# The dense residual moved from the end of the second expert pass to its start, and new places in the order of the delta-rule stage

## The chip, the cores and the metric

The kernel runs on one core of one Trainium2 chip. The metric is the time of one execution on the device, in microseconds (us). A trace of one profiled execution gives every instruction with its start, its length and what its engine waited for.

## The reference

One step of a decoder trunk for 528 prompt tokens (16 of them learned meta tokens) and 8 sequences of 4 new tokens, 560 token columns in all, width 1024, all in fp32:

```
h = h + W_out(concat[GDN(xn), Conformer(xn)])        xn = RMSNorm(h)
h = h + PEER(RMSNorm(h))                             16384 single-neuron experts
y = RMSNorm(h, final_norm_w)                         meta tokens dropped
PEER:  act = gelu(x . u[e]);  y = sum over heads, top 16:  gate * act * v[e]
```

GDN is a gated delta rule with 4 heads of 128, done in chunks: in each a unit triangular system of 128 x 128 is solved per head, with a state matrix handed from chunk to chunk. Conformer is a gated depthwise convolution of 31 taps with a layer norm. PEER scores 128 x 128 product keys in 8 heads and takes the best 16 of each.

## The kernel before, in words

Engines: TensorE (PE) multiplies, VectorE (DVE) and ScalarE (ACT) read its results from PSUM (8 banks), GpSimd (POOL) helps and issues gathers, SyncE (SP) issues all other DMAs in program order.

**Projections and delta stage (to about 457 us).** Weights come in blocks; each is split into a high and a low fp32r part and multiplied in three products. From the ninth block on, the projections share the engines with the delta stage: five chunks (chunk 0 of 48 rows, chunks 1 to 4 of 128 rows, `tile(ci)`), the sample sequences (`sample_tile`), the layer norm (`norm_tile_conf`), the outputs (`outs`, `roots`, `onbs`) and the mix into the operand of `W_out` (`mix_tile`). Each of them is a generator that yields a step's name before it issues the step. `side_by_side` always goes on with the generator whose next step has the smallest time of `turn`, which reads the tables `FIRST`, `HEAD`, `LEVEL`, `SAMPLE_AT`, `OUT_AT`, `NORM_AT` and `MIX_AT`. So each engine has its own written order, and each engine executes strictly in that order. These times are planning units, not us; steps of one generator never overtake each other. The same times deal out the PSUM banks: `GROUPS` is sorted by `turn` and walks round a ring of 4 banks, then 6, then 4. A step that takes over a bank waits until the bank's last group was read (`free_bank`). Between delta steps, DVE has the conformer's convolution to do (`conv_to`, 120 instructions of line 1943), dealt out by the same times (`feed`).

Names used below. `gb` makes the decay arguments, and ACT's two `Exp` per head follow it. `k` transposes a chunk's keys; DVE scales them (KH) and ACT makes RA and KE from them (`ke`). `khT` and `KHT`: the scaled keys transposed and copied. `kk` and `kq`: products of keys and queries. `n2`, `r1`, `nt2`, `nt4`, `r2`, `r3`: steps of the triangular solve, `nt2` and `nt4` being copied by ACT. `wT`, `ws`, `qs`, `su`, `o1`: the chunk's use and update of the state. `sw`, `ktm`, `su00` to `su31`: the sample sequences' states SS, four heads. `li`, `lm`, `ln`: inverse root, multiplication and SiLU of the layer norm. `cl`: low part of the mix on DVE. `oss`, `root`, `onb`, `on`: mean square, root, scaling and transpose of an output chunk. `high` is ACT's high part of the first `W_out` block, and POOL makes the low part (line 848).

**Pass 1 (lines 1294 to 1307).** 416 of the 544 output tokens are dense: for them PE multiplies with all 16384 experts, 128 steps of 24 matmuls of 128 x 416. ACT applies gelu and SP stores to DRAM. The other 128 tokens gather their 128 experts each: POOL gathers rows of u, DVE takes dot products (line 2461). Beside it DVE makes one-hots and PE builds the dense tokens' gate matrix (`gate_batch`). POOL makes the low part of each weight step (line 862).

**Pass 2 (lines 1309 to 1325).** 128 steps of 24 matmuls add activations times v into all 8 PSUM banks, `bank[dt]` holding columns of width 128 x 416 tokens. ACT and DVE prepare the operands (AR, WS) four steps ahead.

**End (lines 1328 to 1337).** The 8 banks hold y transposed. ACT and DVE copy them to yT in turn. PE then puts the residual into each bank: a matmul of an identity with h2, a row tile of 104 tokens by 512 columns, 8 in all. Then it adds yT transposed, 32 matmuls with an identity, 8 for each of the 4 row tiles. Each row tile goes through a mean square (ACT), small steps of DVE and ACT, the scaling (DVE) and its store. The residual's rows and `final_norm_w` are read from DRAM at step 16 of pass 2.

The order around the pass change is that of the engines' programs: the first step of pass 2 waits on `a_low` and `v_low`, and, bank by bank, for the gates, for the dot products and for the last gelu.

## Time and profile before

| | us |
|---|---|
| median of 3 runs | 1844.85 |
| the 3 runs | 1844.85, 1849.69, 1838.57 |
| the profiled execution | 1842.69 |
| its span, first to last instruction | 1840.9 |
| PE busy / DVE busy / ACT busy / POOL busy | 1777.0 / 1384.3 / 712.9 / 681.8 |

Matmuls are pipelined: an instruction's mean length (say 273 ns) is not its pitch. The pitch is the time from a group's start to the next group's, divided by the number of instructions. An fp32 matmul is two rows in the trace, a transpose one row. "Idle before" names the instruction whose end freed the waiting engine.

### The profile page before, as it was taken

What the parts mean: (1) busy time and instruction counts of PE and PEld (TensorE: products, weight loads), DVE (VectorE), ACT (ScalarE), POOL (GpSimd) and SP (SyncE); (2) the same over time, 40 slices, a digit from 0 to 9 for tenths busy, and PEclk for the clock granted to TensorE, in tenths of its full rate; (3) what the DMA queues carried; (4) which work ended last, traced back from release to release, by engine and by line L of the source; (5) the groups of instructions that cost most, each with busy time, mean ns of one, the idle gap of its engine ahead of it and who ended that gap; (6) DMA issues with size and microseconds to landing.
All of it is one profiled execution on the core that took longest, in us unless ns stands there. A gap on an engine that the chain in (4) does not pass through costs nothing.

```text
span 1840.9 us, 29413 instructions
## 1 busy us (share of the span) xinstructions
PE 1777.0 (97%) x11497; PEld 1728.0 (94%) x11497; DVE 1384.3 (75%) x2533; ACT 712.9 (39%) x1244; POOL 681.8 (37%) x448
## 2 busy tenths in 40 slices
PE   7999987979999999999999999999999999999998
PEld 6998886879999999999999999999999999999997
DVE  4887887674899999999865665437697888887752
ACT  4546325453333334443433333333233333333332
...
GB/s 215 69 47 43 36 5 49 24 150 124 118 47 111 218 275 264 295 294 311 300 322 293 308 313 318 289 378 354 338 402 374 339 347 361 342 342 355 293 118 38
DMA packets 190706, 424.33 MB, mean 231 GB/s; under 512 B 11162, under 2 KB 119222, under 8 KB 180320
## 3 DMA queue, kind: packets, MB, share of 16 engines
...
## 4 chain that ended last, share of the span: by engine, by line
PE 75%; DVE 19%; ACT 3%; issue 2%; POOL 1%; DMA 0%; SPq 0%; DVEq 0%; ACTq 0%; POOLq 0%
PE psum L1321 32%; PE psum L1300 21%; PE psum L927 9%; PE psum L1288 3%; PE psum L922 3%; DVE cT L1943 2%; DVE junk L2461 2%; PE psum L1030 2%; PE psum L1078 1%; DVE besti L2336 1%; DVE oh L2451 1%; DVE besti L2324 1%; DVE sring L2328 1%; DVE eqx L2394 1%; DVE pick L2399 1%
## 5 line engine op out<-in xcount | busy, mean ns | idle before, releaser
L1300 PE MATMUL psum<-xT,WS 128*128 128x416 f32 x3072 | 594.8, 353 | 2.8 <-POOL WS L862 2.7
L1321 PE MATMUL psum<-AR,WS 128*128 128x416 f32 x3072 | 582.1, 351 | 2.6 <-DVE AR L2532 2.6
L1321 PEld LDWEIGHTS psum<-AR,WS 128*128 128x128 f32 x3072 | 575.6, 188 | 9.0 <-DVE AR L2532 3.0
L1300 PEld LDWEIGHTS psum<-xT,WS 128*128 128x128 f32 x3072 | 572.2, 188 | 8.5 <-POOL WS L862 4.0
L862 POOL TENSOR_TENSOR WS<-RAWP,WS 128x1024 fp32r<-128x1024 f32 x128 | 310.9, 2439 | 315.6 <-ACT WS L1730 215.0
L853 POOL DMA_INDIRECT rowg<-in_expert_v,idx x128 | 182.0, 1422 | 317.6 <-DVE acc L2475 309.7
L927 PE MATMUL psum<-xT,WR 128*128 128x280 f32 (+2 forms) x1968 | 272.0, 296 | 4.7 <-DVE WR L1830 3.3
L1740 ACT ACTIVATE WS<-RAWP 128x1024 fp32r<-128x1024 f32 x128 | 135.6, 1059 | 336.2 <-PE psum L1321 325.9
L927 PEld LDWEIGHTS psum<-xT,WR 128*128 128x128 f32 x1968 | 258.1, 191 | 6.6 <-DVE WR L1830 3.6
L2525 DVE TENSOR_TENSOR WS<-RAWP,WS 128x1024 fp32r<-128x1024 f32 x128 | 156.5, 1223 | 116.2 <-ACT WS L1740 116.2
L1767 ACT ACTIVATE actA<-psum 128x416 f32<-128x416 f32 x128 | 66.3, 518 | 401.8 <-PE psum L1300 395.5
L2461 DVE CUSTOM_DVE_ANT_0 junk<-rowg,psum 128x1024 bf16<-128x1024 f32 x128 | 155.9, 1218 | 51.8 <-DMA rowg<-in_expert_u_rows,idx 43.8
L853 POOL DMA_INDIRECT rowg<-in_expert_u_rows,idx x128 | 166.0, 1297 | 37.6 <-issue 22.7
L2475 DVE SCALAR_TENSOR_TENSOR acc<-rowg,coef,acc 128x1024 f32<-128x1024 f32 x128 | 163.8, 1279 | 3.2 <-DMA rowg<-in_expert_v,idx 1.0
L2451 DVE TENSOR_TENSOR oh<-iotab,pairs 128x2048 bf16<-128x2048 bf16 x52 | 93.7, 1801 | 93.0 <-PE psum L1288 92.2
L1730 ACT ACTIVATE WS<-RAWP 128x1024 fp32r<-128x1024 f32 x128 | 134.5, 1053 | 0.0
L1943 DVE SCALAR_TENSOR_TENSOR cT<-gext,dwcols,cT 128x528 f32<-128x528 f32 x120 | 92.3, 769 | 4.2
L840 POOL MEMSET WQP<- 128x2048 f32 x1 | 1.8, 1809 | 246.9 <-PE psum L927 246.9
L2454 DVE TENSOR_TENSOR ohg<-oh,pairs 128x3072 bf16<-128x3072 bf16 x52 | 91.5, 1759 | 1.8
L2523 DVE TENSOR_TENSOR act<-act,Gt 128x416 f32<-128x416 f32 x128 | 74.9, 585 | 12.7 <-DMA act<-act_dram 9.1
L1792 ACT ACTIVATE AR<-act 128x416 fp32r<-128x416 f32 x128 | 69.0, 539 | 36.9 <-DVE act L2523 36.9
L2532 DVE TENSOR_TENSOR AR<-act,AR 128x416 fp32r<-128x416 f32 x128 | 74.9, 585 | 7.3 <-ACT AR L1792 7.3
...
## 6 DMA issues: line engine op xcount, KB each, us to landing
...
act_dram<-actA SPq DMA_DIRECT2D x128, 208.0 KB
...
```

Of the source, the lines that this page charges most:

```text
L853: pool.indirect_dma_start(out=rowg[:, s_ % 4, :], out_offset=None, in_=table, in_offset=bass.IndirectOffsetOnAxis(ap=idx[:, s_ % PAIRS:s_ ...
L862: pool.tensor_tensor(ws(n)[:, 1], raw(n), ws(n)[:, 0].bitcast(F32), ALU.subtract).then_inc(u_low, 1)
L927: last = mm(bank[u % 4][:, 0:hw], W[:, pw, kt, m * P:(m + 1) * P], xT[:, px, kt, c0:c0 + hw], **go)
L1300: last = mm(bank[e % 2][:, 0:TD], ws(e)[:, pw, kt * P:(kt + 1) * P], xT[:, px, kt, TSP:TPE], start=(kt == 0 and i == 0), stop=(kt == KT - ...
L1321: last = mm(bank[dt][:, 0:TD], ws(NK + e)[:, pw, dt * P:(dt + 1) * P], AR[:, e % 4, pa, :], start=(e == 0 and i == 0), stop=(e == NK - 1 a ...
L1730: act.activation(ws(n)[:, 0], raw(n), ACT.Copy).then_inc(u_high, 1)
L1740: act.activation(ws(n)[:, 0], raw(n), ACT.Copy).then_inc(v_high, 1)
L1943: op(dve.scalar_tensor_tensor(d, x, w, d, ALU.mult, ALU.add))
L2451: chain(tt(by_two(oh[:, i]), keys_, per_token(0, 2), ALU.is_equal))
L2461: dve.tensor_tensor_reduce(junk[:], rowg[:, s_ % 4, :], xnP, 1.0, 0.0, ALU.mult, ALU.add, sdot[:, s_:s_ + 1]).then_inc(dot_done, 1)
L2475: dve.scalar_tensor_tensor(acc[:], rowg[:, s_ % 4, :], coef[:, s_:s_ + 1], acc[:], ALU.mult, ALU.add).then_inc(axpy_done, 1)
L2525: tt(ws(NK + e)[:, 1], raw(NK + e), ws(NK + e)[:, 0].bitcast(F32), ALU.subtract).then_inc(v_low, 1)
```

## The change

Two things are changed, and nothing of what is computed.

**Residual.** PE now writes h2 of the dense tokens into the 8 banks before pass 2 adds to them: for each bank and row tile one matmul with 104 x 128 rows of h2 as the weights and a 104 x 104 identity as the moving operand, 32 matmuls. Those of 6 banks stand ahead of the first step's waits, those of banks 0 and 1 inside that step. The rows are loaded by 4 DMAs of 416 KB at step 100 of pass 1, into places that are free by then. At the end the 8 residual matmuls are gone, and the 32 matmuls with an identity have become 32 transposes.

**Order of the delta stage.** On ACT, chunk 0's exponentials come after its `khT` copy, and chunk 4's after chunk 3's `ke`. `su20` and `su21` come after `nt2` of chunk 4. The layer norm's `li1`, `lm` and `ln` come later, and so do the `cl`. The mean square of output chunk 3 goes from DVE to ACT, and later in the order.

Not shown in the diff: the semaphore `hd_in`, and `hf[:, 0, :]` become `hf[:]` in four places.

```diff
@@ -84,6 +84,7 @@
 G2_AT = GATE_END + 7
+HD_AT = 100
 DOTS_PRE, DOTS_IN, GATHER0 = 14, 102, 14
...
@@ -363,11 +364,13 @@
         sq2 = at("sq2", [P, D], F32, w_rowg + 2 * D)
-        assert used["e"] <= room - D
+        hrest = at("hrest", [P, D], F32, used["e"])
+        hcols = at("hcols", [P, 2 * KT, NT], F32, w_xT)
+        assert used["e"] + D <= room - D and P <= TSP
         yoT = at("yoT", [P, 3, D], F32, w_Gt)
-        hf = at("hf", [P, NTP, D], F32, w_xT)
-        yT = at("yT", [P, KT, TD], F32, w_xT + NTP * D)
-        assert NTP * D + KT * TD <= 2 * KT * NT
+        hf = at("hf", [P, D], F32, w_xT)
+        yT = at("yT", [P, KT, TD], F32, w_xT + D)
+        assert D + KT * TD <= 2 * KT * NT
...
@@ -424,8 +428,9 @@
         FIRST = {0: 4.2, 1: 12.5, 2: 27.9, 3: 41.3, 4: 43.6}
-        HEAD = {"gb": {0: -2.4, 1: -2, 2: -2.4, 3: -1.2, 4: -1.28}, "k": {0: -1.3, 1: -0.8, 2: -0.7, 3: -0.2, 4: -0.8},
-                "ke": {0: -0.9, 1: -0.1, 2: -0.3, 3: 1.05, 4: -0.4}, "su": {0: 9.1, 1: 14, 2: 14, 3: 14, 4: 14.15}}
+        HEAD = {"gb": {0: -2.4, 1: -2, 2: -2.4, 3: -1.2, 4: -1.2},
+                "exp": {0: 1.05, 1: -2, 2: -2.4, 3: -1.2, 4: -1.2}, "k": {0: -1.3, 1: -0.8, 2: -0.7, 3: -0.2, 4: -0.8},
+                "ke": {0: 1.1, 1: -0.1, 2: -0.3, 3: 1.05, 4: -0.4}, "su": {0: 9.1, 1: 14, 2: 14, 3: 14, 4: 14.15}}
         END_AT = 54.65
...
@@ -438,15 +443,16 @@
             SAMPLE_AT[f"su{hh}0"], SAMPLE_AT[f"su{hh}1"] = 50.2 + 1.2 * hh, 50.25 + 1.2 * hh
-        OUT_AT = {"oss": {SAMPLE: 46.5, 1: 46.6, 2: 46.7, 3: 55.45, 4: 57.82},
+        SAMPLE_AT["su20"], SAMPLE_AT["su21"] = 52.92, 52.94
+        OUT_AT = {"oss": {SAMPLE: 46.5, 1: 46.6, 2: 46.7, 3: 56.62, 4: 57.82},
                   "root": {SAMPLE: 46.8, 3: 56.65, 4: 58.02},
                   "onb": {SAMPLE: 48.9, 1: 50.1, 2: 51.1, 3: 56.68, 4: 58.05},
                   "on": {SAMPLE: 49.6, 1: 50.7, 2: 51.7, 3: 57.8, 4: 58.95}}
         NORM_AT = {"ls": 48.5, "lc": 48.55, "sq0": 49.3, "sq1": 49.35, "lv0": 50.3, "lv1": 50.8, "sq2": 50.85,
-                   "lv2": 51.3, "sq3": 51.32, "lv3": 51.75, "lr": 51.85, "li0": 52.2, "li1": 52.45}
+                   "lv2": 51.3, "sq3": 51.32, "lv3": 51.75, "lr": 51.85, "li0": 52.2, "li1": 52.87}
         for c in range(NG):
-            NORM_AT[f"lm{c}"], NORM_AT[f"ln{c}"] = 52.5 + 0.2 * c, 52.6 + 0.2 * c
-        MIX_AT = {"conformer": 53.8, "cl0": 54.0, "cl1": 54.2, "cl2": 54.4, "cl3": 54.6, "high": 54.8, "table": 55.65,
+            NORM_AT[f"lm{c}"], NORM_AT[f"ln{c}"] = 52.95 + 0.25 * c, 53.31 + 0.25 * c
+        MIX_AT = {"conformer": 54.1, "cl0": 54.2, "cl1": 54.35, "cl2": 54.5, "cl3": 54.65, "high": 54.8, "table": 55.65,
                   "out0a": 57.85, "out1a": 57.9, "out2a": 57.95, "delta": 57.96, "deltalow": 58, "out0b": 58.6,
...
@@ -547,6 +553,12 @@
             return yo[:, t, :] if t < 2 else yoT[:, t - 2, :]
+
+        def dense_rows(t):
+
+            if t <= 2:
+                return hcols[0:DB, KT * (t - 1):KT * t, 0:P]
+            return (wrow if t == 3 else hrest)[0:DB, :].rearrange("p (k n) -> p k n", k=KT)
...
@@ -725,6 +737,12 @@
                     load_pair(e // 2 + 4)
+                if e == HD_AT:
+                    V.wait(sp, "pairs", ND)
+                    sp.wait_ge(h2_done, 32)
+                    for t in range(1, NTP):
+                        sp.dma_start(dense_rows(t), h2_dram[t, 0:DB, :].rearrange("p (k n) -> p k n", k=KT)
+                                     ).then_inc(hd_in, 16)
                 if e in GSTORE_AT:
...
@@ -760,10 +778,9 @@
                     sp.wait_ge(s_mm, NK)
+                    T.wait(sp, "hT")
                     load_row(final_norm_w.rearrange("(a d) -> a d", a=1), row_in[2])
-                    sp.dma_start(hf[:, 0, :], h2_dram[0]).then_inc(hf_in, 16)
-                    sp.dma_start(hf[0:DB, 1:NTP, :], h2_dram[1:NTP, 0:DB, :].rearrange("t p d -> p t d")
-                                 ).then_inc(hf_in, 16)
+                    sp.dma_start(hf[:], h2_dram[0]).then_inc(hf_in, 16)
                 if e == AX_END + 12:
...
@@ -1305,36 +1322,44 @@
+            def residual(dt):
+
+                if dt == 4:
+                    pe.wait_ge(hd_in, 64)
+                    pe.wait_ge(gate_bank, 2 * NBAT)
+                    V.wait(pe, "pairs", ND)
+                elif dt == 2:
+                    pe.wait_ge(dot_done, PAIRS)
+                elif dt == 0:
+                    pe.wait_ge(gelu_done, NK)
+                for t in range(1, NTP):
+                    last = mm(bank[dt][:, (t - 1) * DB:t * DB], dense_rows(t)[:, dt, :], ident[0:DB, 0:DB],
+                              start=(t == 1), stop=False)
+                return last
+
+            for dt in (4, 5, 6, 7, 2, 3):
+                residual(dt)
             for e in range(NK):
                 pe.wait_ge(a_low, e + 1)
                 pe.wait_ge(v_low, e + 1)
                 for dt in ((4, 5, 6, 7, 2, 3, 0, 1) if e == 0 else range(KT)):
-                    if e == 0:
-                        if dt == 4:
-                            pe.wait_ge(gate_bank, 2 * NBAT)
-                            V.wait(pe, "pairs", ND)
-                        elif dt == 2:
-                            pe.wait_ge(dot_done, PAIRS)
-                        elif dt == 0:
-                            pe.wait_ge(gelu_done, NK)
+                    if e == 0 and dt < 2:
+                        T.op(residual(dt), "hT")
                     for i, (pw, pa) in enumerate(((0, 0), (0, 1), (1, 0))):
                         last = mm(bank[dt][:, 0:TD], ws(NK + e)[:, pw, dt * P:(dt + 1) * P], AR[:, e % 4, pa, :],
-                                  start=(e == 0 and i == 0), stop=(e == NK - 1 and i == 2))
+                                  start=False, stop=(e == NK - 1 and i == 2))
                     if e == NK - 1:
                         last.then_inc(y_bank, 1)
                 if e < NK - 1:
                     last.then_inc(p_mm, 1)
 
-            pe.wait_ge(hf_in, 32)
             for d in range(KT):
-                t, i = 1 + d // 2, d % 2
                 (A if d % 2 else V).wait(pe, "yT", d)
-                mm(bank[d][0:DB, :], ident[0:DB, 0:DB], hf[0:DB, t, 512 * i:512 * i + 512], start=True, stop=False)
             for t in range(1, NTP):
                 for j in range(KT):
-                    last = mm(psum[0:DB, 1024 * (t - 1) + j * P:1024 * (t - 1) + (j + 1) * P],
-                              yT[:, j, (t - 1) * DB:t * DB], ident[:], start=False, stop=j % 4 == 3)
+                    last = pe.transpose(psum[0:DB, 1024 * (t - 1) + j * P:1024 * (t - 1) + (j + 1) * P],
+                                        yT[:, j, (t - 1) * DB:t * DB], ident[:])
                 T.op(last, "y", t)
...
@@ -1528,16 +1553,14 @@
-                yield "gb", ci
-                V.wait(act, "arg", ci)
-                for hh in range(HEADS):
-                    fn(M[6][0:c, hh, 0:c], M[6][0:c, hh, 0:c], ACT.Exp, bias=row_of(GCB, c, ci, hh), scale=-1.0)
-                    fn(M[5][0:c, hh, 0:c], M[5][0:c, hh, 0:c], ACT.Exp, "exp", ci, bias=row_of(NGC, c, ci, hh),
-                       scale=1.0)
-                if ci == len(CHUNKS) - 2:
-                    yield "khT", ci
-                    take("khT", KHT[:, :, 0:c], P)
-                    yield "ke", ci
+                def exps():
+                    V.wait(act, "arg", ci)
+                    for hh in range(HEADS):
+                        fn(M[6][0:c, hh, 0:c], M[6][0:c, hh, 0:c], ACT.Exp, bias=row_of(GCB, c, ci, hh), scale=-1.0)
+                        fn(M[5][0:c, hh, 0:c], M[5][0:c, hh, 0:c], ACT.Exp, "exp", ci, bias=row_of(NGC, c, ci, hh),
+                           scale=1.0)
+
+                def keys():
                     V.wait(act, "k", ci)
...
@@ -1545,15 +1568,26 @@
                     each_head("ke", lambda hh: KE[0:c, hh, :], of_head("k"), lambda hh: row_of(RKE, c, ci, hh), ci)
+
+                if ci == 0:
+                    yield "khT", ci
+                    take("khT", KHT[:, :, 0:c], P)
+                    yield "exp", ci
+                    exps()
+                    yield "ke", ci
+                    keys()
+                elif ci == len(CHUNKS) - 2:
+                    yield "exp", ci
+                    exps()
+                    yield "khT", ci
+                    take("khT", KHT[:, :, 0:c], P)
+                    yield "ke", ci
+                    keys()
                 else:
+                    yield "exp", ci
+                    exps()
                     yield "ke", ci
-                    V.wait(act, "k", ci)
-                    if ci == 1:
-                        T.wait(act, "r0b", 0)
-                    if ci == 0:
-                        V.wait(act, "qconv", 3 * HEADS - 1)
-                    each_head(None, lambda hh: RA[0:c, hh, 1, :], of_head("k"), lambda hh: row_of(RKB, c, ci, hh), ci)
-                    each_head("ke", lambda hh: KE[0:c, hh, :], of_head("k"), lambda hh: row_of(RKE, c, ci, hh), ci)
+                    keys()
                     yield "khT", ci
...
@@ -1610,7 +1644,7 @@
-                for i, ci in enumerate(OUTS[:-2]):
+                for i, ci in enumerate(OUTS[:-1]):
                     tc, c = (0, TS) if ci == SAMPLE else (ci, P)
...
@@ -2162,7 +2196,7 @@
                     yield "oss", ci
-                    if ci in OUTS[-2:]:
+                    if ci == OUTS[-1]:
                         squares = SETS[SET[ci]]["RB"][:, :, 0, :]
...
@@ -2532,8 +2566,8 @@
                     dve.wait_ge(axpy_done, PAIRS)
-                    dve.wait_ge(hf_in, 32)
-                    op(tt(hf[:, 0, :], hf[:, 0, :], acc[:], ALU.add), "hf", 0)
+                    dve.wait_ge(hf_in, 16)
+                    op(tt(hf[:], hf[:], acc[:], ALU.add), "hf", 0)
                 if e == AX_END + 6:
```

## Rows read from the trace of the kernel before

**Rows 1.** The page, costliest groups: line, operation | busy us, mean ns | idle before, releaser
```profile
L1300 PE MATMUL psum<-xT,WS 128*128 128x416 f32 x3072 | 594.8, 353 | 2.8 <-POOL WS L862 2.7
L1321 PE MATMUL psum<-AR,WS 128*128 128x416 f32 x3072 | 582.1, 351 | 2.6 <-DVE AR L2532 2.6
```
**Rows 2.** Chain of waits, the end: start us, length us, what
```profile
1819.76 6.87 PE psum L1333 x16
1826.63 1.76 PE psum L1336 x16
...
1831.47 0.07 DVE fs L2562
...
1833.28 0.07 DVE fs L2562
```
**Rows 3.** Timeline, the last copy of yT on ACT
```profile
1819.80 0.52 ACT L1343 ACTIVATE yT<-psum 128x416 f32<-128x416 f32 x1 [0.62 <-PE psum L1321]
```
**Rows 4.** Chain of waits: 16 transposes of 128 x 128; 6 matmul rows of one column
```profile
445.33 1.75 PE psum L1229 x16
...
128.00 0.61 PE psum L976 x6
```
**Rows 5.** Chain of waits, the change of the passes
```profile
1214.83 20.25 PE psum L1300 x107
...
1237.68 7.48 PE psum L1321 x30
```
**Rows 6.** Windows after the pass change: stretch, its us, busy of each engine, PEclk, DMA share
```profile
1237.70:1240.00 2.30, 2.30 (x9) 2.23 (x10) 2.30 (x4) 0.56 (x1) 0.00 (x0) 0.72 1.06 422
1240.00:1244.00 4.00, 4.00 (x17) 3.89 (x17) 4.00 (x7) 1.10 (x2) 0.00 (x0) 0.74 1.01 405
```
**Rows 7.** Timeline of DVE in pass 1, about step 100
```profile
1110.30 1.27 DVE L2451 TENSOR_TENSOR oh<-iotab,pairs 128x2048 bf16<-128x2048 bf16 x1 [4.96 <-PE psum L1288]
```
**Rows 8.** Timeline of PE, head of chunk 0
```profile
146.53 0.88 PE L1047 MATMUL psum<-KHT 128*48 128x48 f32 x8 [3.13 <-ACT KHT L1343]
```
**Rows 9.** Timeline of ACT, PE, DVE and SP's queue, heads of chunks 3 and 4
```profile
286.05 0.60 ACT L1343 ACTIVATE KHT<-psum 128x512 f32<-128x512 f32 x1 [1.99 <-PE psum L1044]
290.20 2.44 ACT L1343 ACTIVATE M<-M,tok 128x128 f32<-128x128 f32 x8 [3.55 <-DVE M L2082]
...
294.82 1.09 PE L1042 MATMUL psum<-ident,kC 128*128 128x128 f32 x4 [6.03 <-ACT KE L1343]
...
300.98 0.69 DVE L2088 TENSOR_TENSOR M<-psum,M 128x512 f32<-128x512 f32 x1 [3.53 <-PE psum L1047]
305.44 0.67 DVE L2191 TENSOR_TENSOR UVM<-UVM,psum 32x512 f32<-32x512 f32 x1
...
288.94 1.04 SPq L641 DMA_DIRECT2D SS<-in_state_gdn  x2
```
**Rows 10.** Windows, as group 6: clock and DMA after that idle time; DVE beyond
```profile
294.00:295.00 1.00, 0.18 (x1) 0.21 (x2) 0.00 (x0) 0.68 (x3) 0.00 (x0) 0.50 0.07 14
...
300.00:320.00 20.00, 16.48 (x140) 15.24 (x138) 18.29 (x27) 9.58 (x39) 0.00 (x0) 1.00 0.00 1
```
**Rows 11.** Timeline of PE, DVE and POOL, solve of chunk 4 to the first output block
```profile
373.87 2.04 PE L1030 MATMUL psum<-M,M 128*128 128x128 f32 x8 [4.89 <-ACT M L1343]
380.90 1.16 PE L1110 MATMUL psum<-state,M 128*128 128x128 f32 x8
...
385.66 0.68 DVE L2250 TENSOR_TENSOR xT<-cT,xT 128x512 fp32r<-128x512 f32 x1
...
388.30 3.00 DVE L2168 TENSOR_TENSOR RB<-vC 128x512 f32<-128x512 f32 x1
395.93 0.69 DVE L2144 TENSOR_TENSOR state<-state,psum 128x512 f32<-128x512 f32 x1 [1.91 <-ACT state L1343]
...
398.04 0.69 DVE L2168 TENSOR_TENSOR RB<-vC 128x512 f32<-128x512 f32 x1
...
386.22 4.53 POOL L848 TENSOR_TENSOR WR<-RAW,WR 128x2048 fp32r<-128x2048 f32 x1 [108.20 <-ACT WR L1343]
```

5 lines of the change are left out of this document (3 added, 2 removed).

## Prediction

> **What bounds the kernel now.** I read the page first. The two expert passes are 1177 us of the span, and PE waited only 2.8 and 2.6 us in them [rows 1]. They can be made shorter only at their edges. So next I read the chain of waits at the end, where PE runs 16 rows of residual matmuls after its last product [rows 2], and at the pass change, where one gap of 2.6 us lies [rows 5]. The windows behind that gap show that PE's clock is not full there [rows 6]. Then I read each engine's timeline in the delta stage. There no engine is full, and it is the written order that makes them wait for each other: look for a PE idle time whose releaser had itself stood behind something else. There are three, of 3.13, 6.03 and 4.89 us [rows 8, 9, 11], and the diff moves just what stood in front.
>
> The sum is made against the profiled execution: 1842.7 us, with a span of 1840.9. The median of the runs is 2.2 above it (1844.85), and the three runs spread over 11 us.
>
> **A1. The end.** Before: the last product ends at 1819.76, the residual takes 6.87, and 16 rows of identity matmuls for row tile 1 take 1.76, to 1828.39 [rows 2]. After: only the copy of bank 7 stands between. It starts at 1819.80 and takes 0.52 [rows 3]; with the hand-over PE starts at about 1820.4. Row tile 1 then needs 8 transposes. In a stream 16 of them took 1.75, so 0.109 each [rows 4], 0.9 in all, to 1821.3. Gain 7.1. The bounds are 6.2 (a transpose as dear as the two matmul rows that it replaces) and 7.2. Row tiles 2 to 4 follow at 1.81 each (1831.47 to 1833.28 [rows 2]). That is the loop of DVE and ACT; PE needs less per tile now and did before, so nothing more comes of it.
>
> **A2. The pass change.** Added are 32 fp32 matmuls, 64 rows, 128 weight columns and 104 moving ones. No row has this shape. The cheapest neighbour has one moving column and the same weights: 0.61 for 6, so 0.10 [rows 4]. The dearest near one is the identity matmul of 128 columns, 1.76 for 16, so 0.11 [rows 2]. I take 0.105: 48 rows are 5.0 us and the 16 inside step 0 are 1.7. The first 48 can start when pass 1 ends, 1235.08 [rows 5]: their waits (gates, last dot product, rows of h2) are long met. So they end at 1240.1. Step 0 began at 1237.68 [rows 5], and its operands do not depend on PE, so it is 2.4 late. With the 1.7 PE is 4.1 late (3.7 to 4.7 with the two neighbours), and as pass 2 is PE throughout, all of it reaches the end.
>
> Against that stands the clock. After the idle 2.6 us the granted clock is 0.72 and 0.74 over 2.3 and 4.0 us [rows 6]: that is 3.4 us at 1.2 instead of 2.4 GHz, a loss of 1.7. The gap is filled now, so I take the 1.7 back (bound 0, if the small matmuls don't keep the clock up). Net cost of A2: 2.4, bounds 2.0 and 4.7.
>
> A1 and A2 together: 4.7 gained, between 1.5 and 5.2.
>
> **A3. The moved loads.** 4 DMAs of 416 KB leave step 16 of pass 2 and go onto SP's queue at step 100 of pass 1, before the gate store. Their waits are met there, the pair loads run four pairs ahead, and issuing costs SP some 0.5 us each. At some 400 GB/s [rows 6] 1.7 MB are 4 us of all DMA engines, so gathers may come later and hold DVE's dot products. But DVE waits 4.96 us for PE before its one-hots [rows 7]. I take nothing; bounds: 2 lost (one late gate batch), and nothing to gain, as PE hardly waits in either pass.
>
> **B1. Head of chunk 0.** ACT did 8 exponentials, RA and KE before the KHT copy, and PE waited 3.13 for that copy [rows 8]. Now the copy comes first, PE gets it some 2.4 earlier, and the exponentials are done just when `kk` needed them before. But ACT has the same work and now idles those 2.4 us waiting for PE's projection half, so its next copies come only some 0.7 earlier. I take 0.7 (bounds -0.5 and 1.5).
>
> **B2. Heads of chunks 3 and 4.** KHT is copied at 286.05; ACT then idles 3.55 for chunk 4's arguments, does its exponentials at 290.20 (2.44), and only then chunk 3's RA and KE, for which PE waits until 294.82 [rows 9]. The clock is at 0.50 by then [rows 10]. After: RA and KE at 286.7 to 288.8, chunk 4's keys on PE at 288.9, `sw1`, then `kk` of chunk 3 at 291.3 to 292.2. DVE's line 2088 comes at 292.5 and not at 300.98 [rows 9]. What is late next is the sample sequences: `sw2` and `sw3` need the states that SP asks for at 288.94 [rows 9]. The DMAs are quiet from 294 [rows 10], so `sw3` ends at about 297, and DVE's line 2191 follows at 297.3 and not at 305.44 [rows 9]. From there DVE is nearly full (18.3 of 20 us [rows 10]), with the same work in the same order, so the 8.2 are kept. Bounds: 3 (below, rival 3) and 9.
>
> **B3. Solve of chunk 4 to the first output block.** PE waits 4.89 for the `nt2` copy, which on ACT stood behind two `ln` that waited for DVE's `lm` [rows 11]. After: `n2`, `r1`, `nt2` on PE to 366.3, `su20` and `su21` to 368.3, and `nt2` is copied at 366.4, so `nt4` runs at 368.8 and not at 373.87. DVE does `r1` before `li1`, and its `ktm3` ends at about 373.5; PE waits some 2 us for it. Then `ws` of chunk 3 comes at 375.4 and not at 380.90 [rows 11]. Of these 5.5 DVE takes some back: `lm`, `r2`, `su30`, `su31` and the `cl` now press on it, and I get `o1` of chunk 3 only 3 us earlier. Then a DVE instruction of 3.00 (mean square, line 2168) and its reduction leave [rows 11], against some 1.3 of squares on ACT and a table load that DVE did not see before. I find chunk 4's `su` at 391.4 and not at 395.93 [rows 11]: 4.5, bounds 0 and 5.5. What follows it (last output block, query blocks, passes) is released by it and moves along.
>
> Sum: 4.7 + 0.7 + 8.2 + 4.5 = 18.1. From 1842.7 that is 1824.6, from the median 1826.8. I say 1826.
>
> **Where the skill speaks against it.** Line 2168 took 3.00, though the same at 398.04 takes 0.69, and it ended 0.55 after POOL's 4.53 us instruction [rows 11]: a DVE instruction that reads its two inputs from SBUF stood still while POOL worked. The Trainium skill, GPSIMD Engine Reference, section Key points, says that GpSimd shares its SBUF interfaces with VectorE and contends with instructions that have two SBUF inputs. By that rule the trace agrees, and it makes rival 1 below.
>
> The last transposes run with no product beside them. The Trainium skill, TensorE: Matmul & The Clock Gate, Part 4, says that transposes do not count as activity for the clock. If that let the clock fall at once, the 8 of tile 1 would take twice as long and the sum would be 17.2; no row of before has transposes alone.
>
> **Rivals.**
> 1. *The `cl` collide with POOL.* Before, the last `cl` began at 385.66, POOL at 386.22 [rows 11]. After, I find the `cl` at 382.6 and POOL at 382.8. If POOL comes first, `cl3` waits for its end, some 4 us, and `r3`, `wT` and all of chunk 4 behind it. For: POOL moves with ACT's `high`, nearly as much as DVE. Against: it is 0.2 us on the right side. B3 gives 0.5, the total is 14.1: 1830 to 1831.
> 2. *The rows of h come late.* They are asked for after `su31`, so only some 3 us earlier, while the output block wants them 4.5 earlier, and the DMA share there is high. It would give back up to 3: 1829.
> 3. *B2 only moves the wait.* If the wait for the states lets the clock fall before `sw2` and `sw3`, these 3.6 us take 7.2 and line 2191 comes at 302: B2 gives 3, the total is 13: 1831 to 1832. Against: PE works until 293.
> 4. *The new order is worth nothing*, since DVE with its convolutions is the bound anyway. Then A alone is left: 1838 to 1840, within 0.5%. Against: DVE itself idles 3.5 us right before line 2088 [rows 9].
> 5. *Slower: the residual's matmuls do not overlap.* Place: the pass change. If a matmul that changes its weights each time has the pitch of the 512-column residual, 6.87 over 16 or 0.43 [rows 2], the 64 cost 27.5, less the 2.6 of the gap and the 7.1 of the end: A loses 17.8, and with B's 13.4 the kernel is 4.4 slower: 1847. It decides from a pitch of 0.36. Against: 0.10 and 0.11 in [rows 2, 4], with new weights each time.
>
> **Numbers.** Forecast as summed 0.60, its own range 1821 to 1830. Rival 1: 0.15, rival 2: 0.08, rival 3: 0.08, rival 4: 0.07, rival 5: 0.02. 0.5% is 9.2 us, about what a measurement of this kernel can tell from none. The first four cases lie beyond it but for their upper tails (0.91 in all, less 0.03 of these), rival 4 within. Faster 0.88, same 0.10, slower 0.02. The range 1820 to 1837 leaves out rival 5, most of rival 4, and the tails that the runs' spread of 11 us gives.
>
> **What would show it.** A1: no residual between the last product and the transposes, and ACT's first square about 1.6 us after the last product. A2: PE without a gap from pass 1 to pass 2, 48 rows in about 5 us, clock 1.00 behind. B1: PE waits under 1 us for KHT. B2: PE's keys of chunk 4 right behind `sw0`, DVE's line 2191 some 11 us behind chunk 3's KHT copy (before, 286.05 to 305.44: 19.4 [rows 9]). B3: no 4.89 us before `nt4`, ACT squares for chunk 3, no 3.00 us instruction on DVE. The prediction is wrong if the time from chunk 3's KHT copy to the first output block does not shrink, if a `cl` takes 3 us or more, or if PE waits in pass 1 at the steps after 100.

## The result, and the profile after

The changed kernel is 1.44% faster: the ratio of its time to the time before is 0.9856, with a 95% interval of 0.9831 to 0.9880. The medians are 1817.3 us (1815.53 to 1819.79, 4 runs) and 1841.84 us (1838.57 to 1849.69, 4 runs). The forecast was 1826 with a range of 1820 to 1837. The direction was right, but the gain came out larger: 22.8 us between the two profiled spans (1840.9 and 1818.1), 24.5 between the medians, and 18.1 in my sum. The time lies below the range. The forecast was made from 1844.85, the median of the first three runs of before; a fourth run brought it to 1841.84, so the gain is larger even against the lower base.

First the page, costliest groups of after. The columns are those of [rows 1].
```profile
L1317 PE MATMUL psum<-xT,WS 128*128 128x416 f32 x3072 | 594.7, 353 | 2.8 <-POOL WS L879 2.8
L1349 PE MATMUL psum<-AR,WS 128*128 128x416 f32 x3072 | 574.2, 348 | 0.0
```
The products of pass 1 are unchanged. Pass 2 has no idle time any more, but look at the busy time: 574.2 for the same 3072 products that took 582.1 in [rows 1]. The forecast had 1.7 us for that.

The chain of waits of after at the change of the passes and at the end (start us, length us, what):
```profile
1189.88 33.29 PE psum L1317 x176
1223.17 5.34 PE psum L1336 x48
1228.51 3.38 PE psum L1349 x18
1231.89 0.87 PE psum L1336 x8
...
1799.85 3.94 PE psum L1349 x21
...
1803.81 0.53 ACT yT L1368
...
1804.47 1.07 PE psum L1361 x8
...
1805.57 1.12 ACT sq L1368 x2
```
The residual (L1336) stands between the passes, 48 rows and then twice 8. Step 0 begins 5.34 us after the end of pass 1. Behind the last product only a copy and 8 transposes are left; ACT's square starts 1.78 us after the last product. Before it was 8.65 (1828.41, right behind the transposes of [rows 2]).

The delta stage of after, timelines of ACT, PE and DVE (start us, us, engine, line, what, count, idle before and its releaser):
```profile
141.87 0.33 ACT L1368 ACTIVATE KHT<-psum 128x192 f32<-128x192 f32 x1 [0.68 <-PE psum L1061]
...
143.50 0.56 PE L1064 MATMUL psum<-KHT 128*48 128x48 f32 x8
...
283.41 0.60 ACT L1368 ACTIVATE KHT<-psum 128x512 f32<-128x512 f32 x1 [1.98 <-PE psum L1061]
284.91 1.17 ACT L1368 ACTIVATE KE<-psum,tok 128x128 f32<-128x128 f32 x4
...
286.23 0.63 PE L1059 MATMUL psum<-ident,kC 128*128 128x128 f32 x4
290.65 3.71 PE L1157 MATMUL psum<-SS,WQP 128*64 128x128 f32 x32
...
294.40 0.68 DVE L2225 TENSOR_TENSOR UVM<-UVM,psum 32x512 f32<-32x512 f32 x1
...
316.61 5.73 PE L1198 MATMUL psum<-cT,ones 128*128 128x280 f32 x16 [2.72 <-DVE cT L1977]
...
359.24 1.06 PE L1047 MATMUL psum<-M,M 128*128 128x128 f32 x8
...
372.61 0.68 DVE L2284 TENSOR_TENSOR xT<-cT,xT 128x512 fp32r<-128x512 f32 x1
382.03 0.69 DVE L2178 TENSOR_TENSOR state<-state,psum 128x512 f32<-128x512 f32 x1 [1.91 <-ACT state L1368]
384.14 0.69 DVE L2202 TENSOR_TENSOR RB<-vC 128x512 f32<-128x512 f32 x1
...
373.47 4.54 POOL L865 TENSOR_TENSOR WR<-RAW,WR 128x2048 fp32r<-128x2048 f32 x1 [98.07 <-ACT WR L1368]
```
The three idle times of [rows 8, 9, 11] are gone: PE's `kk` of chunk 0 waits for nothing, the keys of chunk 4 (L1059) come at 286.23 and not at 294.82, and `nt4` (359.24) waits for nothing.

So the two profiles add up as follows. Each line is one instruction or boundary that both have.

| point | before | after | earlier by | step | its gain | forecast |
|---|---|---|---|---|---|---|
| KHT copy of chunk 3 | 286.05 | 283.41 | 2.6 | B1 (run-in 0.2 later) | 2.8 | 0.7 |
| DVE on the sample's UVM | 305.44 | 294.40 | 11.0 | B2 | 8.4 | 8.2 |
| first `lc` on DVE | 332.14 | 322.38 | 9.8 | nothing of the change | -1.3 | 0 |
| `su` of chunk 4 | 395.93 | 382.03 | 13.9 | B3 | 4.1 | 4.5 |
| end of pass 1 | 1235.08 | 1223.17 | 11.9 | A3 | -2.0 | 0 |
| last product | 1819.76 | 1803.79 | 16.0 | A2 | +4.1 | -2.4 |
| end of span | 1840.9 | 1818.1 | 22.8 | A1 | 6.8 | 7.1 |

Three terms are off: B1 by 2.1, A3 by 2.0 the other way, and A2 by 6.5 (6.8 of pitch, less 0.4 by which the rows were dearer). Another 1.3 was lost at `ls` (the layer norm's sums on PE), where the clock had fallen. A2 is what took the time out of the range: with the 6.8 us back in it, the median of 1817.3 would have been 1824.1.

### The profile page after: what moved, and what is told of

Its sections match the earlier page's. It is cut to its first block, busy times and chain, and to the rows that moved or that the text cites. A ratio compares the mean times of both kernels' runs of the same rounds, so it can differ in the third digit from the quotient of the medians.

```text
span 1818.1 us, 29460 instructions
## 1 busy us (share of the span) xinstructions
PE 1763.9 (97%) x11513; PEld 1722.9 (95%) x11513; DVE 1382.6 (76%) x2531; ACT 713.9 (39%) x1252; POOL 676.6 (37%) x448
## 4 chain that ended last, share of the span: by engine, by line
PE 74%; DVE 18%; issue 2%; ACT 2%; DMA 2%; POOL 1%; SPq 0%; DVEq 0%; ACTq 0%; POOLq 0%
PE psum L1349 32%; PE psum L1317 20%; PE psum L944 10%; PE psum L1305 3%; PE psum L939 3%; DVE cT L1977 2%; DVE junk L2495 2%; PE psum L1047 1%; DMA gate_dram<-gblk 1%; PE psum L1095 1%; DVE oh L2485 1%; DVE besti L2370 1%; DVE besti L2358 1%; DVE sring L2362 1%; DVE eqx L2428 1%
## 5 line engine op out<-in xcount | busy, mean ns | idle before, releaser
L1349 PE MATMUL psum<-AR,WS 128*128 128x416 f32 x3072 | 574.2, 348 | 0.0
L870 POOL DMA_INDIRECT rowg<-in_expert_v,idx x128 | 176.6, 1380 | 320.0 <-DVE acc L2509 312.2
L1305 PEld LDWEIGHTS psum<-ohg,oh 128*128 128x128 bf16 x1248 | 70.1, 98 | 11.1 <-issue 11.1
L1305 PE MATMUL psum<-ohg,oh 128*128 128x128 bf16 x1248 | 78.7, 219 | 1.8 <-ACT gblk L1816 1.8
## 6 DMA issues: line engine op xcount, KB each, us to landing
gate_dram<-gblk SPq DMA_DIRECT2D x26, 1024.0 KB, 10.5
```

Of the source, the lines that this page charges most:

```text
L870: pool.indirect_dma_start(out=rowg[:, s_ % 4, :], out_offset=None, in_=table, in_offset=bass.IndirectOffsetOnAxis(ap=idx[:, s_ % PAIRS:s_ ...
L1305: last = mm(bank[4 + g % GBANKS][:, k * NK:(k + 1) * NK], oh[:, b % 2, 0, i, :], ohg[:, b % 2, x, i, :], start=(x == 0), stop=(x == 2))
L1349: last = mm(bank[dt][:, 0:TD], ws(NK + e)[:, pw, dt * P:(dt + 1) * P], AR[:, e % 4, pa, :], start=False, stop=(e == NK - 1 and i == 2))
```

## The experiments

Pass 2 first. In both traces I took the distances between the starts of the products. They repeat with a period of three. In before it is 188, 193, 186 ns (each 1 ns up or down), mean 188.9. In after it is 189, 183, 188 ns, mean 186.7, from the second product of step 0 on. Each holds from early in pass 2 to its end. 2.2 ns times 3072 are 6.8 us. From step 1 on, the two kernels issue the same products there, from the same buffers. I call it the slower and the faster cadence. A window of 100 us shows it too: in 1500 to 1600 us the first row below (before) has 531 products, the second (after) 538, and PE is busy all the time in both. The columns are those of [rows 6].
```profile
1500.00:1600.00 100.00, 100.00 (x531) 99.00 (x531) 81.39 (x94) 33.58 (x44) 37.04 (x27) 1.00 0.93 351
```
```profile
1500.00:1600.00 100.00, 100.00 (x538) 99.73 (x537) 81.24 (x93) 34.21 (x46) 35.72 (x27) 1.00 0.95 357
```

**a_only, b_only: each half of the change alone.** In `a_only` the times and orders of the delta stage are the old ones, in `b_only` only they are new. The diff is that of the change, cut in two:
```
a_only:  -"exp": {...}, NORM_AT, MIX_AT, OUT_AT as before;  +residual(dt), dense_rows(t), HD_AT
b_only:  the reverse
```


> Only the residual is changed (its rows at the change of the passes, transposes at the end, the loads of h moved); the delta stage is in the old order. My sum gave 4.7 us for this part: 1837 to 1838. Theory now, from the trace of after: the 3072 products of pass 2 have a shorter pitch there (186.7 instead of 188.9 ns), which is 6.8 us that I had not counted, and the moved loads lose 1.9. Then the gain against before is 8.5 to 9.5 us in the span and PE's products of pass 2 take 574 us, not 582. Rival: the shorter pitch came with the new delta stage or is the chip's scatter; then the gain is 2 to 5.

> Only the delta stage is in the new order; the residual stays at the end as before. My sum gave 13.4 us, the two traces give 13.5 to 14 (2.7 at the head of chunk 0, 8.4 at the heads of chunks 3 and 4, 1.7 lost again in front of `ls`, 4.2 from chunk 4's solve to the first output block). Theory: span shorter by 13.5 to 14, PE's products of pass 2 at 582 us as before. Rival (the shorter pitch belongs to this part): 20 us shorter and 574.

Measured: `a_only` has a ratio of 0.9936 (0.9919 to 0.9952), a median of 1833.2 and a span of 1833.7. From the start of pass 1 to the end it takes 1256.3 us (before 1265.4): 9.1 gained. (The span is only 7.2 shorter, since pass 1 began 1.9 later.) The products of pass 2 take 574.2 us and start some 5 us after pass 1, with the clock at 1.00 between (window of `a_only`, columns as in [rows 6]):
```profile
1239.00:1243.90 4.90, 4.90 (x47) 4.90 (x46) 3.13 (x5) 2.49 (x5) 0.00 (x0) 1.00 1.02 413
```
`b_only` has 0.9913 (0.9885 to 0.9941), a median of 1829.1 and a span of 1825.6, 15.3 shorter than before. Its `su` of chunk 4 comes at 379.52, 16.4 earlier than before's. 0.9 of that was there before the stage began, and its `ls` ran at full clock, so the stage itself gains 15.5 (expected 13.5 to 14), which is after's 14.1 and most of the 1.7 that after lost at `ls`. Its pass 2 started in the faster cadence, and then something unforeseen came; the chain of waits of `b_only` at step 21:
```profile
1288.36 30.18 DMA act<-act_dram
...
1321.49 0.51 DVE AR L2543
...
1322.05 3.04 PE psum L1323 x9
```
A load of activations was 30 us on its way. The 2.1 MB of rows of h, asked for at step 16, were under way beside it. PE stopped for 2.0 us, the clock fell, and behind the stop the cadence was the slower one to the end. So the faster cadence is not the property of one half's code, and neither the theory nor the rival held for `b_only` as written. In eight of the nine kernels that have the new residual and no forced stop, the products of pass 2 take 574.2 us on the page; in the ninth (`hd120`, below) the clock was half at their start, and they take 575.8.

**fill: PE's gap filled with something that is not the residual.**
```
+            for _ in range(24):
+                mm(bank[4][:, 0:104], ident[:], ident[:, 0:104], start=True, stop=True)
             for e in range(NK):                     # pass 2
```


> The kernel before with 24 identity matmuls of 128x104, whose result nothing reads, in PE's gap of 2.6 us between the passes; the residual stays at the end. Theory: what changed the pitch of pass 2 is that PE enters it without idling and at full clock. Then the clock is 1.00 after the change of the passes (gain 1.7), the 3072 products take 574 us (gain 6.8), and the span is 8 to 8.5 us shorter than before. Rival 1: only the clock comes back: 1.7 shorter, products 580 to 581. Rival 2: the small matmuls do not keep the clock up: no gain, up to 0.5 slower.

Measured: 1.0011 (0.9991 to 1.0031), span 1841.3. The 8 us expected did not come. Each of these fp32 matmuls is two rows, so it was 48 rows and 5.5 us, twice the gap, and step 0 was 2.2 us later than before. The clock stayed at 1.00 and pass 2 began in the faster cadence. It stayed so for 21 steps. Then PE stopped for 0.61 us, again at step 21, and the slower cadence followed though the clock was full. Windows of `fill` around the stop:
```profile
1337.00:1339.20 2.20, 1.73 (x10) 1.39 (x8) 2.20 (x3) 0.99 (x2) 0.15 (x1) 1.00 0.86 352
1339.20:1341.00 1.80, 1.66 (x9) 1.64 (x10) 1.80 (x4) 1.18 (x2) 0.91 (x1) 1.00 0.85 304
```
So it is not the clock itself that sets the cadence.

**stall40: one stop forced in pass 2 of after.**
```
-                pe.wait_ge(a_low, e + 1)
+                pe.wait_ge(a_low, e + (4 if e == 40 else 1))
```


> The kernel after, in which PE waits once, in front of step 40 of pass 2, for the operands of step 43 instead of step 40. Theory: the same 24 products of a step run in one of two cadences, 186.7 or 188.9 ns each on average, and the stream keeps the one in which it was started until it is interrupted; a stop with products behind it (and the fall of the clock in it) puts it into the slower one. Then the stop costs its 2 to 4 us, some 1.7 of clock, and the 87 steps behind it have 188.9 ns: 4.6 us more, 8 to 10 longer than after in all. Rival: the cadence belongs to the code of after (addresses, order): 186.7 ns before and behind the stop, 4 to 6 longer.

Measured: 0.9937 (0.9917 to 0.9957), median 1831.2, 13.9 over that of after. In the profiles pass 2 is 586.2 us long instead of 575.5, 10.7 more. PE waited 4.16 us. The clock was at 0.50 for a stretch behind it. The 87 steps behind it have the slower cadence, and they had the faster one ahead of it. Timeline of PE, then windows, of `stall40`:
```profile
1410.93 5.41 PE L1349 MATMUL psum<-AR,WS 128*128 128x416 f32 x19 [4.16 <-DVE AR L2566]
```
```profile
1300.00:1400.00 100.00, 100.00 (x537) 99.71 (x537) 82.12 (x94) 34.45 (x46) 37.04 (x27) 1.00 0.94 357
1412.00:1415.40 3.40, 3.40 (x11) 3.24 (x10) 0.00 (x0) 0.00 (x0) 0.00 (x0) 0.50 0.96 339
1500.00:1600.00 100.00, 100.00 (x532) 98.99 (x531) 80.60 (x94) 33.85 (x46) 37.92 (x28) 1.00 0.95 353
```
537 products in 100 us ahead of the stop, 532 behind it. 4.2 + 1.7 + 87 x 24 x 2.2 ns = 10.5 of the 10.7 us. (The median is 3 us more over that of after, which one profile does not explain.) The rival (one cadence for one code) has fallen.

**reset24: eight small rows in pass 2 of before.**
```
+                if e == 24:
+                    for _ in range(4):
+                        mm(bank[0][:, TD:512], ident[:], ident[:, 0:512 - TD], start=False, stop=False)
```


> The kernel before with four identity matmuls (8 rows) into unused columns of bank 0 in front of step 24 of pass 2. In after, the same sort of rows stand in step 0, and behind them the pitch is 186.7 ns even where the clock had fallen just before. Theory: steps 1 to 23 keep their 188.9 ns, steps 24 to 127 run at 186.7: 5.5 us shorter, less 0.9 for the rows, so 4 to 5 shorter than before. Rival 1: 188.9 throughout, since the small rows do not set it; 1 longer. Rival 2: the pitch belongs to what ran beside it.

Measured: the span is 1836.9, 4.0 shorter than before's, and pass 2 alone 4.7 (577.4 instead of 582.1; expected 4.6). The ratio is 0.9987 (0.9977 to 0.9997), so in the medians it is some 2 us. Steps 1 to 23 have the slower, 24 to 127 the faster cadence. Timeline of PE, then windows, of `reset24`:
```profile
1348.79 1.03 PE L1313 MATMUL psum<-ident 128*128 128x96 f32 x8
```
```profile
1250.00:1340.00 90.00, 90.00 (x478) 89.06 (x477) 65.37 (x76) 27.83 (x38) 27.94 (x21) 1.00 0.95 338
...
1500.00:1600.00 100.00, 100.00 (x537) 99.72 (x536) 82.53 (x95) 33.60 (x44) 38.06 (x27) 1.00 0.95 352
```
This is the switch in the other direction, in a kernel that has nothing of the change, with one profile for it.

**loads, loads_reset2, loads_reset1, loads_fill: the pitch alone.** All four are the kernel before with the loads of h taken apart, so that nothing stops pass 2. The other three add 8 rows at step 2, 2 rows there, or 24 rows in the gap between the passes.
```
loads:         -sp.dma_start(hf[0:DB, 1:NTP, :], ...)   at step 16
               +sp.dma_start(hf[0:DB, t, :], ...)       at steps 40, 50, 60, 70
loads_reset2:  +for _ in range(4): mm(bank[0][:, TD:512], ident[:], ...)   before step 2
loads_reset1:  +mm(bank[0][:, TD:512], ident[:], ...)                      before step 2
loads_fill:    +for _ in range(12): mm(bank[4][:, 0:104], ident[:], ...)   before pass 2
```


> The kernel before, with the four loads of the rows of h one by one at steps 40, 50, 60 and 70 of pass 2 instead of together at step 16. Theory: together at step 16 they stand in the same DMA queues as the activations (9 to 11 us in which DVE waits for `act`), and in some executions PE stops at step 21; apart, they stop nobody. The profiled span stays at 1840 to 1842 with 188.9 ns in pass 2 (the cadence comes from the change of the passes), and the runs scatter less upward than before's. Rival: nothing changes at all in either.

> `loads` with four identity matmuls (8 rows) in front of step 2 of pass 2. This is the pitch alone: residual, end and delta stage are those of before. Theory: 126 steps at 186.7 instead of 188.9 ns are 6.7 us, less 0.9 for the rows: 5.8 shorter than before in the span, and as much in the medians, since nothing stops pass 2 any more. Rival: what reset24 gained in its profile but only half of in its median shows that most executions of before do not run at 188.9; then 2 to 3 in the medians.

> `loads` with one identity matmul (2 rows, 0.2 us) in front of step 2 of pass 2, to see how little it takes. If any small matmul between two products starts the cadence afresh: 6.4 to 6.6 shorter than `loads`. Rival: PE must have drained its products for it, which 2 rows do not do: 188.9 ns throughout, 0.2 longer.

> `loads` with 12 identity matmuls (24 rows of 104 columns, 2.7 us) in PE's gap of 2.6 between the passes (the first filling was twice as long as the gap and its pass 2 was stopped at step 21). Theory: the clock stays full, pass 2 begins in the faster cadence and nothing stops it: 1.7 and 6.8, so 8 to 8.5 shorter than before. Rival: without rows between the products the cadence falls to the slower one by itself: 1.7.

| | ratio (95%) | median | span | pass 2 products on the page |
|---|---|---|---|---|
| loads | 0.9992 (0.9975 to 1.0009) | 1842.7 | 1840.9 | 582.1 |
| loads_reset2 | 0.9967 (0.9954 to 0.9980) | 1839.0 | 1839.8 | 575.5 |
| loads_reset1 | 1.0018 (1.0004 to 1.0032) | 1847.1 | 1842.0 | 580.6 |
| loads_fill | 0.9982 (0.9966 to 0.9997) | 1841.7 | 1839.4 | 580.5 |

The groups of pass 2 from the pages of `loads`, `loads_reset2` and `loads_fill`, one fence each:
```profile
L1322 PE MATMUL psum<-AR,WS 128*128 128x416 f32 x3072 | 582.1, 351 | 2.6 <-DVE AR L2533 2.6
```
```profile
L1325 PE MATMUL psum<-AR,WS 128*128 128x416 f32 x3072 | 575.5, 349 | 2.6 <-DVE AR L2536 2.6
```
```profile
L1326 PE MATMUL psum<-AR,WS 128*128 128x416 f32 x3072 | 580.5, 350 | 0.0
```
`loads`: the span and the cadence are as before. DVE's 9.1 us wait for activations is gone from its trace, but the runs show neither a gain nor less scatter. `loads_reset2`: pass 2 is 5.9 us shorter from its first product to its last (576.2 instead of 582.1), against 5.8 expected. The interval of the ratio is 3.7 to 8.5 us. The span is only 1.1 shorter, because in that execution the clock had fallen more often in the first 180 us; pass 1 began 4.7 us later than before's. One thing was not as thought: it had the faster cadence already from late in step 0, so the 8 rows at step 2 changed nothing there. The run shows what the cadence is worth, and not what sets it. `loads_reset1`: two rows did the opposite. It was in the faster cadence up to them and in the slower one behind them, and it came out slower than before (2.0 of that is a longer pass 1, in which PE waited 4.5 us for weights and not 2.7). `loads_fill`: the rival's number came. The clock was full across the change of the passes, PE had no gap, and the cadence was the slower one from the start: 1.5 us gained in the span. But the rival's reason (without rows between the products the cadence falls by itself) does not fit `fill` and `b_only`, which held the faster one for 21 steps without such rows.

So in `loads_fill` the filled gap was worth its clock, 1.5, and nothing more. 8 rows between two products were followed by the faster cadence each time (`reset24`, `loads_reset2`, and step 0 of all kernels with the new residual). Only in `reset24` and in `hd120`, whose clock had just been half, was it not there before them. In after it follows the 48 rows ahead of step 0. The 48 rows of `fill` were followed by it too, the 24 of `loads_fill` were not. A stop in the midst of the products was followed by the slower one each time (`b_only`, `fill`, `stall40`). The first products of pass 2 in kernels without the new residual went either way.

**hd120, spread: where the rows of h are loaded (A3).**
```
hd120:   -HD_AT = 100    +HD_AT = 120
spread:  +HD_AT = {101: 1, 105: 2, 108: 3, 112: 4}   (one row tile each)
```


> The kernel after with the four loads of the rows of h at step 120 of pass 1 instead of step 100, behind the last gate store. Theory: at step 100 they stood in front of a gate store on SP's queue and beside it in the DMA engines (20.2 us to landing, ACT waited 10.0 for its buffer, PE 1.8); now no gate store is held, PE does not wait for `gblk`, and the span is 1.8 to 2 us shorter than after. Rival: the loads then push the activations and gates that step 123 asks for, pass 2 starts late and nothing is gained or up to 2 us lost.

> The kernel after with the four loads of the rows of h one by one at steps 101, 105, 108 and 112 of pass 1, each a step behind a gate store, instead of all at step 100 in front of one. Theory: no gate store is held up by more than one load of 416 KB, ACT's wait for `gblk` falls from 10.0 us to under 5, PE waits no more in pass 1, and the loads of the change of the passes are not pushed as they were from step 120; span 1.8 to 2 shorter than after, pass 1 in 659.6 us. Rival: any load there delays a gate store past its use; then 0 to 1 shorter.

What happened in after: the chain of waits about step 100, then ACT's waits from 1080 to 1120 us (in total, times, longest).
```profile
1092.32 20.16 DMA gate_dram<-gblk
...
1112.56 0.61 ACT gblk L1816
...
1113.30 1.50 PE psum L1305 x24
```
```profile
ACT gblk L1816 <- DMA gate_dram<-gblk: 10.0, 1, 10.0
```
The gate store stood behind the four loads on SP's queue and beside them in the DMA engines. It landed after 20.2 us where the median of the 26 is 10.5. PE waited 1.8 us, the loss that I had named as the bound of A3 and then set to nothing.

`hd120`: 0.9906 (0.9878 to 0.9934), median 1824.7: worse than after. Pass 1 is 1.9 shorter, as expected (659.6 us), but the rival came true as well. The gates of pass 2 were 22 us on their way, and PE waited 2.5 at the change of the passes, with a half clock behind it. Chain of waits, then timeline of DVE and PE, of `hd120`:
```profile
1201.93 22.00 DMA Gt<-gate_dram
```
```profile
1224.03 0.59 DVE L2557 TENSOR_TENSOR act<-act,Gt 128x416 f32<-128x416 f32 x1 [12.49 <-DMA Gt<-gate_dram]
...
1226.31 5.23 PE L1349 MATMUL psum<-AR,WS 128*128 128x416 f32 x18 [2.51 <-DVE AR L2566]
```
`spread`: 0.9853 (0.9835 to 0.9871), median 1816.6, span 1815.6. ACT waits for no gate store, PE waits in pass 1 for nothing but 2.7 us for weights, as in [rows 1], and pass 1 takes 659.6 us. That is the 1.9 us back. Against after it is 2.5 shorter in the span and 0.7 in the medians, which these runs cannot tell apart.

The loads at step 100 do not cost PE something every time. Seven of the profiled kernels have them there, and in all seven ACT waited for a gate store. Only where it waited long did PE wait too:

| | b2_undo | b1_undo | stall40 | lsfill | a_only | after | b3_undo |
|---|---|---|---|---|---|---|---|
| ACT's longest wait for the gate store | 7.2 | 7.3 | 7.9 | 9.5 | 9.8 | 10.0 | 11.0 |
| PE's wait for `gblk` | 0 | 0 | 0 | 1.2 | 1.6 | 1.8 | 2.8 |

PE pays what exceeds some 8.2 us of ACT's wait (an estimate from this table). `hd120`, `spread` and `best` have no such wait of ACT. Pass 1 was at 659.6 and 659.7 us in `b2_undo` and `stall40` as well, and in `b1_undo` it was 661.7 by a longer wait for weights (4.4 us). So the length of pass 1 alone does not prove that `spread` helped; ACT's wait does.

**b1_undo, b2_undo, b3_undo: one part of the delta stage taken back from after.**
```
b1_undo: -"exp": {0: 1.05, ...}, "ke": {0: 1.1, ...}, KHT first   +{0: -2.4, ...}, {0: -0.9, ...}, exponentials first
b2_undo: -"gb"/"exp": {... 4: -1.2}                               +{... 4: -1.28}
b3_undo: -su20, su21, li1, lm, ln, conformer, cl, oss of chunk 3  +their old times
```


> The kernel after with chunk 0's exponentials again ahead of its KHT copy. My sum gave this step 0.7 us; the two traces give 2.7, because ACT idled only 0.7 us and not 2.4 before the copy. Expected: span up to the first `WR` behind it 2.7 later, whole span 2.0 to 2.8 longer than after. Rival: the gain is taken back by what follows (DVE's convolutions): under 1.

> The kernel after with chunk 4's exponentials again ahead of chunk 3's `RA` and `KE` (the time -1.28 instead of -1.2). My sum gave 8.2 us, the traces 8.4 at DVE's triangular step of chunk 3, and 1.7 less behind `ls`, whose clock was halved after and full before. Expected: the 6.03 us idle before `kk` comes back, `ls` takes 4.0 us again, whole span 6.5 to 7 longer than after. Rival: the half clock at `ls` has nothing to do with this step; then 8.4.

> The kernel after with the third group of times undone (su20 and su21, li1, lm, ln, conformer and cl, oss of chunk 3 on DVE): my sum gave 4.5 us, the traces 4.15. Expected: 4 to 4.5 longer than after, with the 4.89 us before `nt4` and the 3.00 us mean square back. Rival 1: only the idle counts and the mean square was hidden: 1.5 to 3.

Measured against after's median of 1817.3: `b1_undo` 1824.6 (+7.3), `b2_undo` 1825.4 (+8.1), `b3_undo` 1823.0 (+5.7). The spans are 8.7, 7.8 and 6.0 longer, where 2.0 to 2.8, 6.5 to 7 and 4 to 4.5 were expected. Part of that lies outside the step undone. Within the stage, between the same two instructions:

- `b1_undo`, from PE's projection at 133 us to a convolution on DVE at 200 us: 72.4 us, 66.8 in after, so 5.5. It was 69.7 in before. The difference between 2.8 and 5.5 is mainly the clock: over the 8 us from 1.5 us ahead of `kk` it was 0.79 on average in before (145 to 153 us), and here it was at 0.57, and the projection unit of 1.8 us took 3.17.
```profile
148.50 0.88 PE L1064 MATMUL psum<-KHT 128*48 128x48 f32 x8 [3.13 <-ACT KHT L1368]
...
149.87 3.17 PE L944 MATMUL psum<-xT,WR 128*128 128x280 f32 x12
```
```profile
147.00:155.00 8.00, 6.50 (x41) 5.81 (x42) 1.72 (x5) 3.95 (x11) 0.00 (x0) 0.57 0.00 0
```
- `b2_undo`, from chunk 3's KHT copy to `su` of chunk 4: 105.2 us, 98.6 in after, so 6.6, as expected. To DVE's work on the sample's UVM it is 19.4 us for 11.0 in after, the 8.4 of the table again. The 6.03 us are back, and `ls` ran at full clock:
```profile
295.39 1.09 PE L1059 MATMUL psum<-ident,kC 128*128 128x128 f32 x4 [6.03 <-ACT KE L1368]
...
328.65 4.04 PE L1198 MATMUL psum<-cT,ones 128*128 128x280 f32 x16 [2.46 <-DVE cT L1977]
```
- `b3_undo`, the same stretch: 102.6, so 4.0 (expected 4 to 4.5). The rest of its 6.0 in the span is mostly A3 once more: PE waited 2.8 for the gate store, and the clock was at 0.50 behind that wait. The 4.89 us and the 3.00 us are back:
```profile
363.57 2.04 PE L1046 MATMUL psum<-M,M 128*128 128x128 f32 x8 [4.89 <-ACT M L1367]
...
377.85 3.00 DVE L2201 TENSOR_TENSOR RB<-vC 128x512 f32<-128x512 f32 x1
375.77 4.53 POOL L864 TENSOR_TENSOR WR<-RAW,WR 128x2048 fp32r<-128x2048 f32 x1 [100.89 <-ACT WR L1367]
```

**lsfill, best: the half clock at `ls`.** In after, `ls` took 5.73 us (316.61 above), 4.04 in before.
```
                 yield "ls", NORM
+                for _ in range(12):
+                    mm(bank[2][:, 0:104], ident[:], ident[:, 0:104], start=True, stop=True)
                 V.wait(pe, "cconv", 2)
```


> The kernel after with 12 identity matmuls (24 rows of 104 columns, 2.7 us), whose result is overwritten, in PE's idle time of 2.72 us in front of `ls`. Theory: after loses 1.7 us because the clock falls in that idle time and `ls` runs at half of it (5.73 us, 4.04 before). Then `ls` takes 4.0 and the span is 1.7 shorter than after. Rival: the clock fell for something earlier, and the fill changes nothing (0, or 0.3 longer if it ends late).

> The spread loads together with the 12 identity matmuls in PE's idle time in front of `ls`. Two of the kernels with the same delta stage had the full clock at `ls` without any filling, so that run told nothing of the filling. Theory: 1.8 to 2 from the loads, and up to 1.7 at `ls` where the clock would have fallen: 2 to 3.7 shorter than after, 1813.5 to 1815.5. Rival: the filling is worth nothing and the loads are: as `spread`.

`lsfill`: ratio 0.9860 (0.9833 to 0.9887), median 1817.0, span 1814.7, and `ls` took 4.04. But so it did in `hd120`, `b_only` and `spread`, which have the delta stage of after unfilled, while `stall40`, which has it too, had 5.73. Whether the clock falls there differs from one execution to the next with the same order. So this run doesn't show that the filling keeps it up; it shows that 24 rows there cost nothing that it can tell. `best` (`spread` with the filling): 0.9856 (0.9835 to 0.9877), median 1817.0, the same as after and `spread`. No version beats after by more than the runs can tell. By its trace `spread` is the one to keep.

## Why the prediction was right or wrong

**A1, right.** 6.8 for 7.1. The 8 transposes took 1.07 and not 0.9, and some 0.1 lay elsewhere. The granted clock was 1.00 from 1804.4 to 1805.6 and the 8 did not take twice as long, so the time of 0.9 lost that I had worked out beside the Trainium skill's rule (TensorE: Matmul & The Clock Gate, Part 4) did not come. The stretch is too short to test the rule itself.

**A2, the step that failed.** Its parts that I could price from rows were right: 48 rows took 5.34 us (5.0), the 16 others 2 x 0.87 (1.7), less the old gap of 2.6 PE was 4.5 late (4.1), and the clock stayed at 1.00. (The bounds of 3.7 and 4.7 do not follow from the two neighbours that I named: 64 rows at 0.61/6 and at 1.76/16 are 6.5 and 7.0 us, so 3.9 and 4.4.) The failing sentence is "as pass 2 is PE throughout, all of it reaches the end", with the clock's 1.7 as the only gain beside it. I took the pace of the 3072 products as fixed, and it was not. From the end of pass 1 to the last product it is 580.62 us instead of 584.68. That is -4.5 for the rows, +1.7 for the clock, and 6.8 or so for the cadence. That one stream has both cadences, and that each can be switched in mid-stream, is shown by `reset24` (8 rows, to 186.7 ns) and `stall40` (a stop, to 188.9); `b_only` and `fill` show the latter unforced. The pace of before and after follows from it, but no run took the 48 rows and the 16 of the change apart. With that term, 1826 would have been 1819.2. By luck the surplus of B1 (2.1) made up for most of what A3 and `ls` lost (3.3); neither was foreseen. In the profile of before it could be seen only as "582.1 in 3072", 189.5 each, with nothing to compare it with but pass 1, whose weights and banks follow another pattern.

**A3, wrong within its bounds: 2.0 lost for 0.** One of my signs of being wrong came with it: PE waited in pass 1 behind step 100. I had 2 us lost as the bound and took nothing, since DVE waited 4.96 us for PE [rows 7]. That was the wrong neighbour. What was late was the gate store that shares SP's queue and the DMA engines, and ACT's buffer with it. `spread`, `best` and `hd120` show it: without the loads at step 100, ACT waits for no gate store and pass 1 is back at 659.6. With them it depends on the execution, as the table of ACT's waits shows.

**B1, the mechanism right, the size too small: 2.8 for 0.7.** I let ACT idle 2.4 us before the KHT copy. It idled 0.68, since one more copy for the convolution now stands ahead of it. And I had left out the clock: in before it was 0.61 and 0.69 from 146 to 151 us, and `kk`, `kq` and the projection unit behind the wait took 0.88, 0.64 and 2.67 us, in after 0.56, 0.44 and 1.81. So 3.13 and 1.4 went, and PE got two new waits of 1.39 and 0.40 (147.55 and 151.22): 2.7 of the 2.8. Where the clock falls further in that wait, as in `b1_undo`, the step is worth 5.5.

**B2, right: 8.4 for 8.2.** I had PE wait for the states until about 294. They had landed, and `sw2`, `sw3` ran at 290.65 without a wait and at full clock. DVE was then the later one. `b2_undo` gives 8.4 to the same instruction, and 6.6 to `su` of chunk 4, since there the clock at `ls` was the full one. Rival 3 has fallen.

**B3, right: 4.1 for 4.5, and 4.0 by `b3_undo`.** The last `cl` began at 372.61 and POOL at 373.47, so rival 1 did not come, with 0.9 us to spare. The output block starts 14.1 us earlier and no rows of h hold it: rival 2 has fallen. The 3.00 us instruction beside POOL came back in `b3_undo`, ending 0.55 us after POOL again, while in after the same line takes 0.69 with POOL at rest. That agrees with the Trainium skill (GPSIMD Engine Reference, Key points).

**Rivals 4 and 5** have fallen with the result. The pitch of the residual is 0.111 us a row, and rival 5 needed 0.36.

The sum was right where a step was the removal of a wait that the trace named (but for the clock behind it in B1), and wrong where it rested on something that "stays as it is": the pace of the products and the landing of a store. The range was too narrow for the same reason. Its lower end had the bounds of the priced steps and nothing for a term that I had not seen.

What stays open is the cause of the two cadences. I have their period, the events that precede a switch and their cost, and not what in the engine sets them, nor how many small rows it takes: 2 and 24 were followed by the slower one, 8 and 48 by the faster. Each kernel has one profile. Open too is why the medians of before and of `reset24` lie closer (2 us) than their profiles (4). Runs without a profile show no cadence, and some of before's may have the faster one.
